# A 13th ring place in the memory of the fifth rounded tile, a written-out loading loop, and one joint gather in a streaming encoder with experts

## The reference

```python
def swiglu(x, w_gate, w_up, w_down):
    return (jax.nn.silu(x @ w_gate) * (x @ w_up)) @ w_down

def moe_swiglu(h, w_router, b_router, w_gate, w_up, w_down):
    t = h.reshape(b * s, d)
    logits = (t @ w_router + b_router).astype(jnp.float32)
    top_vals, top_idx = lax.top_k(logits, TOP_K)
    top_w = jax.nn.softmax(top_vals, axis=-1)
    combine = ...                       # [256, 8], two weights in a row
    for e in range(N_EXPERTS):
        out = out + combine[:, e:e + 1] * swiglu(t, w_gate[e], w_up[e], w_down[e])
```

## Time and profile before

| | us |
|---|---|
| median of 3 runs (1358.28 to 1360.14) | 1358.3 |
| the profiled execution, its own time | 1360.5 |
| its span, first to last instruction | 1358.8 |
| PE busy | 1310.2 (96%) |
| DVE busy | 1247.8 (92%) |
| ACT busy | 965.8 (71%) |
| DMA | 467 MB, 344 GB/s over the span |

### The profile page before, as it was taken

How to read it: one execution, slowest core, us unless ns; L and a number is a source line. 1 busy time by engine, 2 the same in 40 slices (tenths; PEclk the granted TensorE clock), 3 DMA queues, 4 the chain that set the end, 5 groups by cost and what they waited for, 6 DMA issues and landing times.

```text
span 1358.8 us, 17773 instructions
## 1 busy us (share of the span) xinstructions
PE 1310.2 (96%) x6777; PEld 1097.9 (81%) x6777; DVE 1247.8 (92%) x1080; ACT 965.8 (71%) x933; POOL 142.4 (10%) x140
## 2 busy tenths in 40 slices
PE   5999899999998999999999999999999999999997
PEld 4868799998877878888888888888888888888885
DVE  6988998987958689999999999999999998999998
ACT  5465443334546668888878797978888977879885
POOL 5099300000049000000000000000000000000000
PEclk9999899999999989999999999999999999999999
DMA  9971799987662479999999999999999999999993
GB/s 357 391 263 41 281 345 325 344 302 235 239 218 94 156 299 382 359 414 410 403 410 413 406 401 414 405 408 414 410 399 413 406 407 411 413 399 416 412 401 137
DMA packets 140721, 467.12 MB, mean 344 GB/s; under 512 B 8766, under 2 KB 10972, under 8 KB 126300
## 3 DMA queue, kind: packets, MB, share of 16 engines
q1 hardware_dynamic: 140144, 465.90, 88.8%
q10 hardware_dynamic: 492, 0.08, 0.0%
HBM read 464.90 MB, written 1.05 MB: 343 GB/s over the span
## 4 chain that ended last, share of the span: by engine, by line
PE 86%; DVE 9%; ACT 2%; issue 2%; DMA 1%; SPq 0%; DVEq 0%; ACTq 0%
PE bank L2648 7%; PE bank L2630 7%; PE bank L2635 7%; PE bank L2643 7%; PE bank L2631 7%; PE bank L2091 6%; PE bank L2093 6%; PE bank L2092 6%; PE bank L2691 4%; PE bank L2698 4%; PE bank L2693 4%; PE bank L2722 4%; PE bank L2727 3%; DVE ring_sum L1394 2%; DVE raw_low L1682 1%
## 5 line engine op out<-in xcount | busy, mean ns | idle before, releaser
L1682 DVE TENSOR_TENSOR raw_low<-raw,w_hi 128x2048 fp32r<-128x2048 f32 x118 | 266.1, 2284 | 9.9 <-ACT w_hi L840 9.6
L840 ACT ACTIVATE w_hi<-raw 128x2048 fp32r<-128x2048 f32 x118 | 224.5, 1923 | 36.1 <-PE bank L2635 31.3
L795 ACT ACTIVATE w_hi<-raw 128x2048 fp32r<-128x2048 f32 (+1 forms) x54 | 102.1, 1893 | 110.3 <-PE bank L2093 92.4
L1293 DVE TENSOR_TENSOR w_lo<-raw,w_hi 128x2048 fp32r<-128x2048 f32 (+1 forms) x54 | 123.6, 2296 | 21.4 <-ACT w_hi L795 21.2
L2091 PE MATMUL bank<-h_hi,w_hi 128*128 128x256 f32 x416 | 119.0, 286 | 0.8 <-DVE gate_m L1372 0.8
L2092 PE MATMUL bank<-h_lo,w_hi 128*128 128x256 f32 x416 | 117.7, 283 | 0.0
L2093 PE MATMUL bank<-h_hi,w_lo 128*128 128x256 f32 x416 | 117.7, 283 | 0.0
L1682 DVE TENSOR_TENSOR w_lo<-w_raw,w_hi 128x2048 fp32r<-128x2048 f32 x49 | 110.9, 2284 | 1.2 <-ACT w_hi L840 1.0
L2630 PE MATMUL bank<-w_hi,hg_hi 128*128 128x512 f32 x268 | 106.8, 398 | 0.0
L2631 PE MATMUL bank<-w_hi,hg_lo 128*128 128x512 f32 x268 | 105.5, 394 | 0.0
L840 ACT ACTIVATE w_hi<-w_raw 128x2048 fp32r<-128x2048 f32 x49 | 93.5, 1921 | 12.1 <-PE bank L2698 8.5
(11 more groups left out here) (468 smaller groups left out, 3320.8 us busy)
## 6 DMA issues: line engine op xcount, KB each, us to landing
raw<-in_w_ex_down SPq DMA_DIRECT2D x96, 1024.0 KB, 10.8
w_raw<-in_w_ex_gate SPq DMA_DIRECT2D x69, 1024.0 KB, 10.9
raw<-in_w_ex_up SPq DMA_DIRECT2D x65, 1024.0 KB, 10.9
raw<-in_w_ada SPq DMA_DIRECT2D x48, 1024.0 KB, 7.4
raw<-in_w_ex_gate SPq DMA_DIRECT2D x35, 1024.0 KB, 11.7
more_raw<-in_w_ex_up SPq DMA_DIRECT2D x19, 1024.0 KB, 10.2
fifth_raw<-in_w_ex_up SPq DMA_DIRECT2D x19, 1024.0 KB, 10.0
raw<-in_w_in SPq DMA_DIRECT2D x12, 1024.0 KB, 9.6
```

The costliest lines, as they stand in the source:

```text
L795: act_e.activation(w_hi[:, s % SPLIT, 0:words], raw[:, n % RAW, 0:words], ACT.Copy).then_inc(hi_done, 1)
L840: act_e.activation(dst, src, ACT.Copy).then_inc(hi_done, 1)
L1293: dve.tensor_tensor(w_lo[:, s % SPLIT, 0:words], raw[:, n % RAW, 0:words], w_hi[:, s % SPLIT, 0:words].bitcast(F32), ALU.subtract).then_in ...
L1682: dve.tensor_tensor(lo, src, hi.bitcast(F32), ALU.subtract).then_inc(lo_done, 1)
```

## The change

`PAIR_SPLIT` is 4 and `PAIR_RING` is 13. The 1 MB of `fifth_hi` becomes the thirteenth place (`spare_raw`, `spare_low`), with `c_first` as the semaphore of its landings. The places are now handed out by the order of loading: the first 13 loads (`KNOWN`) are the first L units of pair 0, so L down 2 and 3 of step 0 and the first three L gate units of step 1 are loaded ahead of S gate 0, which waits for the first unit's end. From the second pair on unit n waits for n - 13. SP's loop over pairs is a Python loop, written out. The wide and the narrow selection stand side by side in `picked`, and one product with 192 columns gathers for both, in two halves: after S down 0 and after S down 3 of step 3. Its results lie in banks 1 and 2; ACT copies the narrow rows into a free half of `e_act` and the wide ones into `hg_hi`, in four pieces each, and DVE subtracts in four pieces after S gate 0 and S up 0 (before: two after S gate 1 and L down 1). `gather_s` after L down 0 is gone, and `add_up` of step 3 comes after L down 1, not after L down 0. The first pair keeps its separate gathers. ACT's `silu_l` of step 0 waits for `hgs_done` too. `split_l` on DVE changes in the same way as `evacuate_l`.

```diff
@@ -25,8 +25,8 @@
 SPLIT = 3
-PAIR_SPLIT = 5
-PAIR_RING = 12
+PAIR_SPLIT = 4
+PAIR_RING = 13
 UNIT = 2048
@@ -240,13 +240,16 @@
-    def place_of(n):
-        assert n not in ahead_no
-        return n - sum(a < n for a in ahead_no)
-    unit_at = {place_of(n): n for n in range(E * NU) if n not in ahead_no}
-    assert len(number) == E * NU and BODY == 2 * NU and BODY % PAIR_RING == 0 and FIRST_BODY == BODY - 2
+    ring_units = [n for n in range(E * NU) if n not in ahead_no]
+    KNOWN = [number[u] for u in body[0] if u[1] == "L" and number[u] not in ahead_no][0:PAIR_RING]
+    ring_loads = KNOWN + [n for n in ring_units if n not in KNOWN]
+    makes_room = {n: ring_units[m] for m, n in enumerate(ring_loads[PAIR_RING:])}
+    slot_of, turn_of = {}, {}
+    for i, n in enumerate(ring_loads):
+        slot_of[n] = i if i < PAIR_RING else slot_of[makes_room[n]]
+        turn_of[n] = 0 if i < PAIR_RING else turn_of[makes_room[n]] + 1
+    assert all(makes_room[n] == n - PAIR_RING for n in range(len(body[0]), E * NU))
+    assert len(number) == E * NU and BODY == 2 * NU and FIRST_BODY == BODY - 2
...
@@ -278,7 +281,10 @@
         unused.close()
-        fifth_hi = sb("fifth_hi", [P, UNIT], F32R)
+        spare_in = ExitStack()
+        spare_raw = sb("spare_raw", [P, UNIT], where=spare_in)
+        spare_in.close()
+        spare_low = sb("spare_low", [P, UNIT], F32R)
         fifth_in = ExitStack()
...
@@ -497,34 +502,33 @@
-        pair_hi = [w_hi[:, i, :] for i in range(SPLIT)] + [more_hi[:, :], fifth_hi[:, :]]
+        pair_hi = [w_hi[:, i, :] for i in range(SPLIT)] + [more_hi[:, :]]
         ring_raw = [raw[:, (N0 + i) % RAW, :] for i in range(RAW)] + [w_raw[:, i, :] for i in range(SPLIT)] + [
-            more_raw[:, :], fifth_raw[:, :]]
+            more_raw[:, :], fifth_raw[:, :], spare_raw[:, :]]
         ring_low = [raw_low[:, (N0 + i) % RAW, :] for i in range(RAW)] + [w_lo[:, i, :] for i in range(SPLIT)] + [
-            more_lo[:, :], fifth_lo[:, :]]
-        ring_in = [unit_in[(N0 + i) % RAW] for i in range(RAW)] + more_in
+            more_lo[:, :], fifth_lo[:, :], spare_low[:, :]]
+        ring_in = [unit_in[(N0 + i) % RAW] for i in range(RAW)] + more_in + [c_first]
...
-        RAW_TURNS = sum(place_of(n) % PAIR_RING == 0 for n in unit_at.values())
-        assert all(sum(r % PAIR_RING == i for r in unit_at) == RAW_TURNS for i in range(RAW))
+            i, turn = slot_of[n], turn_of[n]
+            return ring_in[i], 16 * (turn + 1 + ((N0 + i) // RAW if i < RAW else i == PAIR_RING - 1))
+        raw_turns = [sum(slot_of[n] == i for n in ring_units) for i in range(RAW)]
...
@@ -630,32 +644,29 @@
-            narrow = []
-            for n, (_, who, kind, s, i) in enumerate(body[0]):
-                if n in ahead_no:
-                    continue
-                if who == "S" and not narrow:
+            for r, n in enumerate(KNOWN):
+                if r < RAW:
+                    wait_freed(N0 + r - RAW)
+                elif r < PAIR_RING - 2:
                     sp.wait_ge(split_used, S0)
-                    load_pair_unit(ahead_no[0], *AHEAD[0][2:], 0)
+                elif r == PAIR_RING - 2:
...
                     load_pair_unit(ahead_no[1], *AHEAD[1][2:], 0)
-                r = place_of(n)
-                if r < RAW:
-                    wait_freed(N0 + r - RAW)
-                elif r < PAIR_RING - 1:
-                    sp.wait_ge(split_used, S0)
-                elif r == PAIR_RING - 1:
                     sp.wait_ge(crossed, len(CROSSINGS))
-                else:
-                    sp.wait_ge(split_used, S0 + unit_at[r - PAIR_RING] + 1)
-                if who == "S" and not narrow:
-                    narrow.append(expert_at(1, 1))
-                load_pair_unit(n, kind, s, i, 0 if who == "L" else narrow[0])
-            with sp.Fori(1, PAIRS) as p:
+                load_pair_unit(n, *body[0][n][2:], 0)
+                if r == RAW:
+                    load_pair_unit(ahead_no[0], *AHEAD[0][2:], 0)
+            narrow = expert_at(1, 1)
+            for n in ring_loads[PAIR_RING:len(body[0]) - len(ahead_no)]:
+                sp.wait_ge(split_used, S0 + makes_room[n] + 1)
+                load_pair_unit(n, *body[0][n][2:], 0 if body[0][n][1] == "L" else narrow)
+            for p in range(1, PAIRS):
                 wide, narrow, old = expert_at(p * 2, 1), expert_at(p * 2 + 1, 1), expert_at(p * 2 - 1, 1)
                 for j, (q, who, kind, s, i) in enumerate(body[1]):
-                    sp.wait_ge(split_used, p * BODY + (S0 + FIRST_BODY - BODY + j - PAIR_RING + 1))
-                    load_pair_unit(FIRST_BODY + j, kind, s, i, old if q == 0 else wide if who == "L" else narrow)
+                    n = FIRST_BODY + (p - 1) * BODY + j
+                    sp.wait_ge(split_used, S0 + makes_room[n] + 1)
+                    load_pair_unit(n, kind, s, i, old if q == 0 else wide if who == "L" else narrow)
             narrow = expert_at(2 * PAIRS - 1, 1)
...
@@ -1088,16 +1099,23 @@
-                act_e.wait_ge(hgl_ready, n * 2 + (half + 1))
-                act_e.activation(hg_hi[:, 4 * half:4 * half + 4, :],
-                                 bank[1 if n > 0 else 6 + half][:, :].rearrange("p (k t) -> p k t", t=P),
-                                 ACT.Copy).then_inc(hgl_high, 1)
+                if n == 0:
+                    act_e.wait_ge(hgl_ready, gathered(n, half, 0))
+                    act_e.activation(hg_hi[:, 4 * half:4 * half + 4, :], bank[6 + half][:, :].rearrange("p (k t) -> p k t", t=P),
+                                     ACT.Copy).then_inc(hgl_high, 1)
+                    return
+                for j in range(2):
+                    both = bank[1 + j][:, :].rearrange("p (k t) -> p k t", t=2 * P)
+                    part = slice(4 * half + 2 * j, 4 * half + 2 * j + 2)
+                    act_e.wait_ge(hgl_ready, gathered(n, half, j))
+                    act_e.activation(rows_in_scratch()[:, part, :], both[:, :, P:P + HALF], ACT.Copy).then_inc(hgs_ready, 1)
+                    act_e.activation(hg_hi[:, part, :], both[:, :, 0:P], ACT.Copy).then_inc(hgl_high, 1)
...
-                act_e.wait_ge(hgs_ready, n + 1)
-                act_e.activation(gs_pack[:, :, 0:HALF], bank[3 if n > 0 else 5][:, :].rearrange("p (k t) -> p k t", t=HALF),
-                                 ACT.Copy).then_inc(hgs_high, 1)
+                act_e.wait_ge(hgs_ready, 4 * n + 1)
+                rows = rows_in_scratch() if n > 0 else bank[5][:, :].rearrange("p (k t) -> p k t", t=HALF)
+                act_e.activation(gs_pack[:, :, 0:HALF], rows, ACT.Copy).then_inc(hgs_high, 1)
                 act_e.wait_ge(hgs_high, 2 * n + 1)
...
@@ -1149,6 +1167,7 @@
                     if u == (p - 1, "S", "down", FINAL, i) and kind == "down":
+                        act_e.wait_ge(hgs_done, p + 1)
                         silu_l(0, i)
...
@@ -2564,23 +2591,35 @@
...
+            def gather(n, half):
+                pe.wait_ge(sell_done, n * 2 + 2)
+                pe.wait_ge(sels_done, n * 2 + 2)
+                for k in range(4 * half, 4 * half + 4):
+                    o = bank[1 + k % 4 // 2][:, (k % 2) * 2 * P:(k % 2) * 2 * P + P + HALF]
+                    for g in range(G):
+                        last = mm(o, y[:, g, k * P:(k + 1) * P], picked[:, g, 0:P + HALF],
+                                  start=k % 2 == 0 and g == 0, stop=g == 1, skip_group_check=True)
+                    if k % 2 == 1:
+                        last.then_inc(hgl_ready, 1)
...
@@ -2763,8 +2802,12 @@
                             down_s(*old, i)
-                            if (s, i) == (FINAL, 1) and p + 1 < PAIRS:
-                                gather_l(p + 1, 0)
+                            if (s, i) == (FINAL, 0) and p + 1 < PAIRS:
+                                gather(p + 1, 0)
+                            if (s, i) == (FINAL, 3) and p + 1 < PAIRS:
+                                pe.wait_ge(hgl_done, gathered(p + 1, 0, 1))
+                                pe.wait_ge(hgs_ready, 4 * p + 3)
+                                gather(p + 1, 1)
...
@@ -2786,6 +2826,9 @@
                         pe.wait_ge(ea_done, 2)
+                    if s == FINAL and p + 1 < PAIRS:
+                        pe.wait_ge(hgl_done, gathered(p + 1, 1, 1))
+                        pe.wait_ge(hgs_ready, 4 * p + 5)
                     for i in range(n):
...
@@ -2802,9 +2845,7 @@
                             add_gate(s)
-                        if i == 0 and s == FINAL and p + 1 < PAIRS:
-                            gather_s(p + 1)
-                        if i == (0 if s == FINAL else 1):
+                        if i == 1:
                             add_up(s)
```

More of the change, by code:

```diff
@@ L535, in trunk_kernel, with gathered, rows_in_scratch @@
         ZEROED = 7 + RH + 2
+        sel = picked[:, :, 0:P]
+        sel_s = picked[:, :, P:2 * P]
+        def gathered(n, half, j):
+            return half + j + 1 if n == 0 else 2 + 4 * (n - 1) + 2 * half + j + 1
```

(6 more changed lines are left out.)

58 lines of the change are left out of this document (30 added, 28 removed).

## The result

The kernel after takes 1379.67 us (median of 4 runs, 1379.09 to 1380.8), the kernel before 1358.47 in the same comparison (1358.28 to 1360.14): a ratio of 1.0155, 95% interval 1.0143 to 1.0168, or 21.2 us more. The profiled execution took 1379.1 us (span 1377.3). The prediction was 1374.4 us in a range of 1364 to 1382. Sign and range held, and so did the mechanism at S up; the middle was 5.3 us low.

A forecast was written before the change was run, and what follows sets the result against it. PE was taken to bound the expert stage, with DVE just fast enough. Four rounded tiles cost 21.8 us and the joint gather saves 5.7, all else nothing: +16.1 on a median of 1358.3 gives 1374.4 us, range 1364 to 1382.

The forecast's parts named there:

- (1): PAIR_SPLIT 5 to 4: ACT rounds later at S down 3, making PE late at S up; 21.8 us lost in all.
- Step 3 ... nothing: Step 3 of each pair: four rounded tiles cost nothing, as DVE gains during 7.1 us of gathers on PE.
- In step 0 of pairs 1 to 3 nothing, or a few tenths: Four tiles' cost there, tightest at L down 0: a margin of 3.02 us against 2.80 of lateness.
- (2): Joint gather of 192 columns: 5.2 us in place of 7.1 in each of 3 pairs, saving 5.7 us in all.
- DVE is recovered to its cap in the next step 0, so I count it in full: After the joint gather: its whole saving of 1.9 us a pair is kept, 5.7 us in all.
- (3): The gather's copies on ACT and DVE in step 3: nothing if the order holds, otherwise up to 2 us for each of 3.
- (4) to (6): Thirteenth place, order of the first 13 loads, SyncE's loop written out: 0 each, the load order 1 us either way.
- The 1352.6 us: Time for the whole kernel by the skill's buffering rule, keeping only the joint gather's saving; the prediction said the trace disagrees.
- B: S up of steps 1 and 2: DVE's later start is made good, only the gather counts, 1352.6 us; chance 0.08.
- C: Step 3: the gather's hand-over stalls PE, 3 x 2 us more, 1380.4 us; chance 0.09.
- E: Whole change neutral, four tiles' cost half made good and the gather giving more: within 0.2%; chance 0.04.
- D: New waits drop TensorE to its lower clock, eight stretches of 3.4 us, 1401 us; sign: clock under 0.99 after 490 us; chance 0.03.

The follow-up runs named there:

- e1_split4: Kernel before with PAIR_SPLIT 4 in place of 5 and nothing else: 1384.91 us, ratio 1.0185.
- e5_best: Kernel after with five rounded tiles, 12 ring places and add_up of the last step back behind L down 0 in every pair: 1354.59 us, ratio 0.9969.
- e9_best2: e5_best with VectorE's gated_l pair one tile earlier and ScalarE's keep_up and silu_s one unit earlier: 1362.45 us, ratio 1.0023.
- e2_split5: Kernel after with five rounded tiles and 12 ring places, the rest of the change kept: 1358.06 us, ratio 0.9986.
- e6_loads: Kernel before with only the new order of first loads and SP's loop written out: 1358.39 us, ratio 0.9997.
- e4_ring12: Kernel after without the thirteenth place (PAIR_RING 12, still four rounded tiles): 1380.87 us, ratio 1.0166.
- e7_split6: e5_best with six rounded tiles and 11 ring places, in place of five and 12: 1357.13 us, ratio 0.9984 to the kernel before.
- e8_gated2: Kernel after with VectorE's gated_l pair issued after the low tile of S down 2, not S down 3: 1375.89 us, ratio 1.0128.
- e10_fill: Kernel after with 11 extra matmuls, results unread, filling PE's gaps around the last turn_s: 1380.26 us, ratio 1.0157.

## Why the prediction was right, and where it was short

**(1) Four rounded tiles: right in mechanism, place and size at S up, short elsewhere.** Predicted 6 x 2.80 + 2 x 2.3 = 21.4 at S up, measured 21.7, with the 0.4 at pair 0's L down 0 as 0.45. Alone (e1_split4) it costs 26.3 and not 21.8. The mis-sized terms were three. "Step 3 ... nothing" failed in the last pair, where 2.7 us are lost at the end: I looked for S up and L down and not at the chain gated_s, turn_s, high_s, low_s that closes the program, which has no work of PE beside it; the clock, which fell there, took 1.3 us of it in after. "In step 0 of pairs 1 to 3 nothing, or a few tenths" came out as 0.5 us in all, at L up 0 and not at L down 0 as read. The third, at nothing by omission, is 1.1 at L gate of step 1 in pairs 1 to 3, where turn_s waits for gated_s of the step before (the rows of L2720 above); these places I had not read.

**(2) The joint gather: right in the passes, over by a quarter in the net.** 0.164 us a pass was predicted and 0.162 measured, 5.2 us against 5.2. That the time half way between two measured widths was right says that it followed the columns; the forecast had no row for it. "DVE is recovered to its cap in the next step 0, so I count it in full" failed: 0.43 us a pair come back as a wait at the next pair's start, and e5_best and e9_best2 showed that it only changes its place. Net 4.2 us in the stage (e5_best), not 5.7.

**(3) Hand-over of the gather's copies: right.** PE has no wait for them in step 3. I had passed over add_up, moved by one L down unit in the last step, and so put it at nothing without a reason: in after it costs at most 0.5 us, but with five tiles it costs 4.3 in the last units of e2_split5's profile, and 3.5 by the medians of e2_split5 and e5_best.

**(4) to (6): right.** Places, order of loads and the written-out loop are worth nothing (e6_loads, e4_ring12). A place more bought nothing; a place less, with the tile that took its memory, cost 2.5 us (e7_split6). The Trainium skill, "Trainium Kernel Development and Optimization", Best Practices, asks to double-buffer so that transfers overlap with computing. By the traces 12 places did that (no wait for a transfer in before), and 11 with six tiles no longer did in full (25 us of ScalarE's waits in e7_split6). The 1352.6 us that the prediction gave by that rule were 27 off.

**The rivals.** B falls: nothing was made good at S up, and e8_gated2 shows VectorE's start passed on one for one. C falls: PE has no wait for the gather's copies. E falls: the change costs 1.6%. D, the clock, falls where I looked for it: through S up the clock stays at 1.00 beside PE's idling of 1.00 and 0.66 us. It holds in one place that I did not look at, the end, where the sign that I had named for it, a clock under 0.99 after 490 us, did show; it costs 1.3 us there by e10_fill's profile (its working was eight places of 3.4 us). The Trainium skill, "TensorE: Matmul & The Clock Gate", section on HAM oscillation, has a kernel whose clock falls again in every round, behind waits for transfers. Here the trace of after shows one fall in the stage, at the end and behind waits for VectorE, and none in the 8 repeated waits at S up.

The sum at fault: +16.1 predicted, +21.4 in the stage. Of the 5.3 missing, 3.1 are the end of pair 3, 1.1 what the gather gave back (-6.6 + 2.0, both with add_up's 0.24 in them, in place of -5.7), 1.0 L gate of step 1, 0.35 S up and pair 0's L down, and -0.3 all else. What stays open: why the last units of e4_ring12 and e2_split5 stay at the lower clock longer than those of after, behind waits of the same length, and what makes the stage begin 488 to 493 us into a profile. How much of the tail's loss is the clock rests on single profiles; no median resolved it.

## What to carry to other kernels

When three engines look full, the buffer whose release the largest waits name sets the lead between them: count how many units back its cap lies, walk from the cap to the first place with no margin, and price one unit there, once a step. Then walk the last step apart from the others: behind the last unit PE has nothing else to do, so a hand-over that is hidden everywhere else counts in full there and can pull the clock down with it. A freed microsecond on the busiest engine is kept only until the next engine's operation is due; look one stretch on before counting it.
